# The order of nine query blocks, and where the masks of their selected keys are made

## What is computed

```
# per block of 128 queries, 8 heads that share one k and one v of width 64
score = sum_h wi[h] * relu(qi[h] . ki)          # the indexer
score = where(causal, score, -inf)
_, idx = top_k(score, 256)                       # each query keeps 256 keys
s = (q . k) / 8;  s = where(selected and causal, s, min)
p = softmax(s);   out = p @ v
```

## Time and profile before

| | |
|---|---|
| median of 3 runs | 4151.41 us (4147.45 to 4155.1) |
| the profiled execution | 4141.83 us, span 4140.0 us |
| PE busy | 3753.0 us, 91% of the span |
| DVE busy | 2171.5 us, 52% |
| ACT busy | 870.9 us, 21% |
| POOL busy | 555.9 us, 13% |
| attention, layer 0 | first score matmul at 472.2 us, last normalization ends at 625.7 |
| attention, layer 1 | first score matmul at 2511.2 us |

### The profile page before, as it was taken

One profiled execution on the slowest core, in us unless ns is written; L12 is line 12 of the kernel. 1 busy time (PEld: TensorE's weight loads), 2 busy tenths in 40 slices (PEclk: granted clock), 3 DMA queues, 4 the chain that ended last, 5 costly groups with the idle time before them and its releaser, 6 DMA issues.

```text
span 4140.0 us, 69037 instructions
## 1 busy us (share of the span) xinstructions
PE 3753.0 (91%) x29136; PEld 2849.3 (69%) x29136; DVE 2171.5 (52%) x4280; ACT 870.9 (21%) x1768; POOL 555.9 (13%) x444
## 2 busy tenths in 40 slices
PE   7999786999979999999889997769999799999995
PEld 4566464887548888888655664548865488888885
DVE  2599835666245243434646996366662542434345
ACT  1345463332010000000113445523320100000000
POOL 0041100000011221212100410000000121212220
PEclk9999897999889999999999998879998899999998
DMA  2001100000111111112210010100001111111121
GB/s 111 26 31 36 43 17 7 3 3 26 62 62 41 41 41 41 41 50 84 77 40 26 31 36 21 35 1 3 3 26 64 60 41 41 41 44 49 41 82 52
DMA packets 43383, 163.67 MB, mean 40 GB/s; under 512 B 5056, under 2 KB 5072, under 8 KB 42720
## 3 DMA queue, kind: packets, MB, share of 16 engines
q1 hardware_dynamic: 27648, 100.68, 7.0%
q0 software_dynamic: 15456, 58.85, 3.9%
HBM read 135.07 MB, written 23.49 MB: 38 GB/s over the span
## 4 chain that ended last, share of the span: by engine, by line
PE 71%; DVE 22%; issue 4%; ACT 2%; POOL 0%; DMA 0%; DVEq 0%; ACTq 0%; POOLq 0%
PE ps L708 38%; PE ps L738 7%; PE ps L657 7%; PE ps L625 6%; DVE arena L1421 5%; PE ps L899 2%; PE ps L887 2%; DVE little L1451 2%; PE ps L912 1%; PE ps L941 1%; DVE arena L1552 1%; PE ps L669 1%; PE ps L635 1%; DVE arena L1318 1%; DVE arena L1554 1%
## 5 line engine op out<-in xcount | busy, mean ns | idle before, releaser
L708 PE MATMUL ps<-arena 128*128 128x261 f32 x4096 | 924.7, 383 | 5.7 <-POOL arena L544 2.9
L708 PEld LDWEIGHTS ps<-arena 128*128 128x128 f32 x4096 | 775.1, 189 | 135.1 <-issue 5.4
L657 PE MATMUL ps<-arena,ring 128*128 128x348 f32 x2304 | 704.1, 465 | 37.4 <-DVE arena L1297 18.9
L708 PE MATMUL ps<-arena,ring 128*128 128x261 f32 x3072 | 705.1, 385 | 22.4 <-DVE arena L1774 22.1
L708 PEld LDWEIGHTS ps<-arena,ring 128*128 128x128 f32 x3072 | 584.2, 190 | 123.1 <-issue 21.3
L657 PEld LDWEIGHTS ps<-arena,ring 128*128 128x128 f32 x2304 | 438.8, 193 | 301.5 <-issue 59.2
L738 PE MATMUL ps<-arena 64*64 64x64 f32 (+1 forms) x13600 | 512.9, 226 | 97.6 <-DVE arena L1506 43.2
L738 PEld LDWEIGHTS ps<-arena 64*64 64x64 f32 x13600 | 467.6, 135 | 141.7 <-DVE arena L1552 48.8
L1276 ACT ACTIVATE aux<-ps 128x522 f32<-128x522 f32 x64 | 38.9, 607 | 1535.0 <-PE ps L708 1535.0
L1363 DVE TENSOR_TENSOR arena<-aux,ps 128x522 f32<-128x522 f32 x160 | 111.8, 699 | 423.1 <-PE ps L708 422.6
L544 POOL TENSOR_TENSOR arena<-ring 128x512 f32<-128x512 f32 x128 | 170.1, 1329 | 1106.9 <-DMA ring<-units 1101.5
(11 more groups left out here) (228 smaller groups left out, 3690.7 us busy)
## 6 DMA issues: line engine op xcount, KB each, us to landing
ring<-units SPq DMA_DIRECT2D x192, 512.0 KB, 3.7
h_scratch<-arena POOLq DMA_DIRECT2D x24, 522.0 KB, 3.2
arena<-h_scratch POOLq DMA_DIRECT2D x24, 522.0 KB, 8.1
arena<-h_in POOLq DMA_DIRECT2D x16, 522.0 KB, 10.2
out<-arena POOLq DMA_DIRECT2D x8, 522.0 KB, 3.1
arena<-att_scratch POOLq DMA_DIRECT2D x2, 2080.0 KB, 8.8
att_scratch<-arena POOLq DMA_DIRECT2D x16, 256.0 KB, 2.9
aux<-rope POOLq DMA_DIRECT2D x2, 1044.0 KB, 12.4
```

The lines of the kernel that those rows point to most:

```text
L657: ins = mm(ps[:, b + s, 0:SW], ring[:, r * D + k * P:r * D + (k + 1) * P], tile(U0, k)[:, slice_(s)], start=(k == 0), stop=(k == KT - 1))
L708: ins = mm(acc_at(n)[:, s], lhs[:, k * P:(k + 1) * P], rhs(k)[:, s * HALF:(s + 1) * HALF], start=(k == 0), stop=(k == KT // 2 - 1))
```

## The change

The masks of blocks 3 to 8 are made in the jobs of blocks 0 to 5, each three blocks ahead; only that of block 2 is made before attention. The jobs run over blocks 0 to 6, then 8, then 7. What went by a block's number (the bank for V and the spread, the place of the row sums, the counts in waits) now goes by its place in the sequence, and the numbers of row maxima done are summed over the jobs. POOL's copies of the mask of block 8 are issued between the stores of blocks 4 and 5 (before, between those of 3 and 4).

```
-        jobs = [(b, g) for b in range(packed) for g in range(4)] + [(packed, 0)]
-        SCORES = 2 * (len(jobs) - 1) + 1
+        sequence = [*range(packed - 1), packed, packed - 1]
+        place = {b: i for i, b in enumerate(sequence)}
+        jobs = [(b, g) for b in sequence for g in range(1 if b == packed else 4)]
         members = lambda b: range(1 if b == packed else 2)
-        ends = lambda u: 0 <= u < len(jobs) and (u + 1 == len(jobs) or jobs[u + 1][0] > jobs[u][0])
+        maxima = [sum(len(members(b)) for b, g in jobs[:u]) for u in range(len(jobs) + 1)]
+        SCORES = maxima[-1]
+        ends = lambda u: 0 <= u < len(jobs) and (u + 1 == len(jobs) or jobs[u + 1][0] != jobs[u][0])
...
-            return 2 * (u - 1) if jobs[u][0] < 4 else 2 * u
+            return maxima[max(u - 1, 0)] if jobs[u][0] < 4 else maxima[u]
...
-                for b in range(NQB):
+                for b in sequence:
                     n = rows(b)
-                    if b == 4:
+                    if b == packed - 3:
                         pool.wait_ge(S["mask_ready"], w.next("mask_ready"))
...
-                        if g == 0 and b >= 2:
-                            pe.wait_ge(S["att_out"], l * NQB + b - 1)
+                        if g == 0 and place[b] >= 2:
+                            pe.wait_ge(S["att_out"], l * NQB + place[b] - 1)
...
-                        if jobs[u - 2][0]:
-                            act.wait_ge(S["att_out"], l * NQB + jobs[u - 2][0])
+                        if u > 5:
+                            act.wait_ge(S["att_out"], l * NQB + place[jobs[u - 2][0]])
...
-                for b in range(FIRST_SEL, packed - 1):
-                    for step in range(7):
-                        make_mask(b, step)
+                for step in range(7):
+                    make_mask(FIRST_SEL, step)
...
-                        for h in (2 * g, 2 * g + 1) if b in (2, 3) else ():
-                            make_mask(packed - 3 + b, h)
-                        if (b, g) == (3, 3):
+                        if b + 3 <= packed:
+                            make_mask(b + 3, 2 * g)
+                            make_mask(b + 3, 2 * g + 1)
+                        if (b + 3, g) == (packed, 3):
                             dve.sem_inc(S["mask_ready"], 1)
...
-                        dve.wait_ge(S["prob_ready"], l * SCORES + (SCORES if b == packed else 2 * u))
+                        dve.wait_ge(S["prob_ready"], l * SCORES + maxima[u])
...
-                        if b or l:
-                            dve.wait_ge(S["att_stored"], 16 * (l * NQB + b))
+                        if place[b] or l:
+                            dve.wait_ge(S["att_stored"], 16 * (l * NQB + place[b]))
```

More of the change, by code:

```diff
@@ L898, in _ @@
                             for r in range(2):
-                                ins = mm(ps[HEAD * r:HEAD * (r + 1), 6 + b % 2, g * P:(g + 1) * P], val[0:kn, kb, :],
+                                ins = mm(ps[HEAD * r:HEAD * (r + 1), 6 + place[b] % 2, g * P:(g + 1) * P], val[0:kn, kb, :],
                                          pt(u, 0 if b == packed else r)[0:kn, kb, :], start=(kb == 0), stop=(kb == b))
@@ L922, in _ @@
                         pe.wait_ge(S["pt_out"], l * NTURN + turned + 1)
-                        sums = stat[:, 8 * (b % 2):8 * (b % 2) + 8]
+                        sums = stat[:, 8 * (place[b] % 2):8 * (place[b] % 2) + 8]
                         for g in range(1 if b == packed else 4):
@@ L1221, in _ @@
                         for r in members(b):
-                            c = 8 * (b % 2) + 2 * g + r
+                            c = 8 * (place[b] % 2) + 2 * g + r
                             x, at = sm[u % 2][r][:, 0:SEL_W[b]], 16 + 2 * (u % 2) + r
@@ L1650, in _ @@
                         b = jobs[u - 1][0]
-                        sums = stat[:, 8 * (b % 2):8 * (b % 2) + (1 if b == packed else 8)]
-                        dve.wait_ge(S["prob_ready"], l * SCORES + (SCORES if b == packed else 2 * u))
+                        sums = stat[:, 8 * (place[b] % 2):8 * (place[b] % 2) + (1 if b == packed else 8)]
+                        dve.wait_ge(S["prob_ready"], l * SCORES + maxima[u])
                         v.reciprocal(sums, sums).then_inc(S["inv_ready"], 1)
@@ L1664, in _ @@
                                     .rearrange("p (g r q) -> p g r q", r=2, q=n)[:, :, r]
-                                do(v.tensor_tensor(att_t[HEAD * r:HEAD * (r + 1), :, 0:n], own(ps[:, 6 + b % 2, 0:P]),
+                                do(v.tensor_tensor(att_t[HEAD * r:HEAD * (r + 1), :, 0:n], own(ps[:, 6 + place[b] % 2, 0:P]),
                                                    own(rinv[:, 0:P]), ALU.mult))
                         else:
-                            do(v.tensor_tensor(att_t, bank4(6 + b % 2), rinv.rearrange("p (g q) -> p g q", g=4),
+                            do(v.tensor_tensor(att_t, bank4(6 + place[b] % 2), rinv.rearrange("p (g q) -> p g q", g=4),
                                                ALU.mult))
```

## The result

Four executions of the changed kernel had a median of 4112.52 us (4112.0 to 4121.28), beside 4149.81 for four of the kernel before (4147.45 to 4155.1): ratio 0.9913, 95% interval 0.9897 to 0.9929. Faster was right; size and range were not. The profiled execution of the changed kernel took 4112.34 us, against 4141.83 before: 29.5 us less.

The account below looks back on a forecast made before the run. PE, idle 37.4 us before attention while DVE makes masks, was taken as the bound. Savings of 24.75, 2.4 and 0.4 sum to 27.5 us, from 4151.4 to 4123.9, rounded to 4124 (chance 0.68); range 4114 to 4135.

Parts of the forecast that it names:

- Part 1: PE's gap before attention: masks of blocks 3 to 6 leave it, start then set by POOL; 24.75 us less in all.
- Part 2: Six masks made inside attention, blocks 0 to 5: scores of (4, 0) 1.2 us earlier per layer, 2.4 us in all.
- L1644 of (1, 3): DVE's instruction in block 1 (L1641 before the change), queued behind mask steps and a normalization: about 1.5 us later.
- (b): Rival: DVE's masks not wholly hidden, jobs of blocks 0, 1, 4 and 5 become later; 4136 us, chance 0.13.
- (c): Rival: slower, attention latency-bound with every mask step between two L1641 on the path; 4177 us, chance 0.04.
- cover: DVE's idle time in blocks 4 and 5, 3.26 us before one L1641, to hide at most 2.6 us of steps.
- Part 3: End of attention, block 8 before block 7: net 0.2 us less per layer, 0.4 in all; bounds +2 to -2.
- the dip: Low clock around 518, after block 3 in layer 0 alone: costs 1.5 us, may go or come, zero in the sum.
- Rival (a): Clock stays high through the shorter gap, or the dip goes: at most 1.6 us per layer; 4119 us, chance 0.13.
- the base of the sum: Starting time for the whole kernel: median 4151.4 us of the runs shown, 9.6 above the profiled execution's 4141.8.
- runs of one kernel: Range term for the whole kernel's time: runs of one kernel lie 4 us from their median.

Follow-up runs that it names:

- e1: The kernel before, unchanged, timed and profiled again: 4144.09 us.
- e14: The kernel before with 11 matmuls of a constant added on PE behind attention in layer 0 alone: 4145.45 us.
- e4: The changed kernel again, no edit: 4119.31 us, ratio 0.9940.
- e11: The changed kernel for the third time, no edit: 4117.07 us, ratio 0.9933.
- e5: The changed kernel with masks 2, 3 and 4 made in the gap, 5 to 8 moved to other jobs: 4127.27 us, ratio 0.9949.
- e3: The kernel before with only the order changed, block 8 before block 7, masks made as before: 4147.37 us, ratio 1.0008.
- e2: The changed kernel with the jobs in the old order, block 8 last, so the mask change alone: 4124.43 us, ratio 0.9948.
- e6: The changed kernel with one unused 768-column DVE scan (1.8 us) more in each job of blocks 4 and 5: 4131.03 us, ratio 0.9961.
- e7: The changed kernel with 14 matmuls of a constant on PE in the gap before attention, both layers: 4126.05 us, ratio 0.9942.
- e12: The changed kernel with 6 constant matmuls in the gap before attention and 11 behind attention, both layers: 4113.69 us, ratio 0.9918.
- e15: The changed kernel with 6 constant matmuls in the gap before attention, and 11 behind attention in layer 0 alone: 4106.14 us, ratio 0.9905.
- e9: The changed kernel with 11 matmuls of a constant on PE behind attention, both layers: 4116.63 us, ratio 0.9928.

## Why the prediction was wrong in size, step by step

The cut of the profiles, in us, from starts of the same instructions. "Before" is the range of three profiles (first, e1, e14) and "changed" of three (first, e4, e11):

```
                                   before           changed         forecast
gap of PE, layer 0                 17.67 to 19.70   6.35            -11.45
gap of PE, layer 1                 19.67 to 19.68   6.35 to 6.36    -13.3
first scores to (4, 0), layer 0    44.25 to 44.71   42.09 to 43.26  -1.2
                        layer 1    43.21 to 44.39   41.29 to 42.49  -1.2
(4, 0) to attention's end, layer 0 107.59 to 109.06 107.07 to 107.09  -0.2
                           layer 1 107.58 to 107.80 107.08 to 107.09  -0.2
attention's end to L1715, layer 0  59.03 to 60.75   60.75 or 69.39   0
                          layer 1  83.72            83.72 to 83.73   0
```

(59.03 is e14's, with its filling.)

By the means of the three profiles each, the edited stretches, from PE's last projection tile to the end of attention in both layers, are 31.0 us shorter: 25.3 in the gaps, 3.6 up to (4, 0) and 2.1 behind it, for 24.75, 2.4 and 0.4. In the first pair of profiles they are 31.8 us shorter, and the stretches that nobody edited 2.3 longer, 2.1 of it from L1715 to the MLP of layer 0 (563.65 for 561.50); hence the 29.5 of the two spans.

**Part 1, the gap.** Right: 11.3 and 13.3 us, set by POOL and not by the masks' 25 us. e5 shows it by adding 10 us of masks, for which PE's gap grew by 0.2 us at most. In executions like e1's, where PE is 2 us sooner, the gain of layer 0 is 13.35; that case wasn't in the sum.

**Part 2, six masks inside.** Right in mechanism and nearly in size, 1.6 us per layer by the means with e3 and e2 taken in (44.3 to 42.7), 1.8 without them, for 1.2. What scatters these times is how long the low clock lasts into attention. With 10.0, 12.4, 13.3 and 15.7 us of it the changed kernel's are 41.29, 42.09, 42.49 and 43.23 us; before, with 10.1, 13.3 and 14.5 us, they are 43.20, 44.39 and 44.69. At equal length (10 or 13.3 us) the change is worth 1.9 us per layer. L1644 of (1, 3) was late by 1.8 us for a forecast 1.5, and blocks 2 and 3 gained it back. Blocks 4 and 5 cost nothing (107.08), so (b) and (c) fall. How much cover was left I overrated, and the form it takes I had wrong (of eight jobs one had none and two 0.18 us, but three more than 1.8): e6's 1.8 us per job cost 4.25 us per layer for the 1 forecast.

**Part 3, the order.** -0.5 to -0.7 us per layer for -0.2 (e2 against e3); small and of the right sign in the profiles, invisible in e3's total.

**The clock.** From (4, 0) to attention's end in layer 0 before took 109.06 us in its first profile and 108.93 in e14's, but 107.59 in e1's, and the changed kernel 107.07 to 107.09 in all three: the dip of before comes and goes, and is worth 1.4 us, as bounded. The clock's fall in the gap of before was read a little late: 0.69 in [459, 460] puts it at 459.4, 4.9 us into the gap, not at 459.7; nothing hangs on it. Rival (a), a clock kept high in blocks 0 and 1, didn't come about in the changed kernel. Its bound of 1.6 us per layer was too low: where e7 did keep the clock high, in layer 0, the scores of (4, 0) came 2.4 to 3.5 us sooner. The fillings lie on the same line as above: 40.77 and 40.80 us with 6.8 us of low clock (e12 and e15, layer 1), and 39.73 with none.

**The step that failed** is the base of the sum: "The median of the runs shown is 4151.4, 9.6 above the profiled execution, and the measured time goes by that". By the rows the changed kernel's profiled execution should have taken 4114.3; it took 4112.34. I had taken the 9.6 us for an offset of timing against profiling that both kernels have. The runs show no fixed one: the changed kernel's first profiled execution was 0.2 us under the median of its set, e1's 0.9 over, e4's at it and e11's 4.2 under. The base was a small sample that sat high, since e1's set gave 4143.5 for 21 executions of the same kernel, and the changed kernel's first four sat low (three at 4112).

The three sets with the changed kernel give 37.3, 24.2 and 30.8 us by medians, and 36.0, 25.4 and 28.4 by means. The means of all its 15 executions and of the 62 of before in the sets up to e12 are 4117.3 and 4145.7, 28.4 apart, for the forecast 27.5. Measured by them, the miss of 11.4 us (4123.9 against 4112.5) is 5.7 of base too high, 4.8 of the first four too low, and 0.9 of the sum.

The range allowed 4 us for "runs of one kernel", where the changed kernel alone covers 4111.8 to 4130.2; that term was too small by half or more. The bounds of parts 2 and 3 and of the dip, all added, would have given 4116.5 to 4132, which is wider than the 4119 to 4130 taken from them and still doesn't reach 4112.5.

That clock steps of 8.6 us (attention's end to L1715) and some 4 us (two later stages) make this spread is shown for the profiled executions. That they also made the first set of before high is inferred, and the chip is an untested rival, since the medians of before in the four later sets, each on another chip, go from 4143.5 to 4147.9. None of its executions above 4150 us left a profile; there is only a slightly lower mean clock in the results of that kernel (0.944 or 0.945 in executions of 4150.9 to 4155.2 us, 0.945 to 0.948 in those below 4146). Why the clock falls at one place in one execution and not in the next stays open, and so does why e3 and e5 stayed within 2.6 and 3.6 us where the changed kernel spread over 18; the fillings of e9 to e15 moved it and didn't fix it.

## What to carry to other kernels

Work taken out of a gap is worth only the distance to the next thing that the engine waits for. Read that one's end before costing the work, and then put other work there, which is free up to that point. Cover must be counted per job, from one instruction that the next stage needs to the following one, not per block. Where a change is worth under one per cent and PE has long half-idle stages, cut several profiles at the same instructions before believing either a median of four or the offset of one profile.

## What the runs showed of the hardware

Two things I hadn't expected. Identical code took 60.75 or 69.39 us in one stage, with a mean granted clock of 0.66 in the first profile and 0.57 in e4's, so PE was at 1.2 GHz for most of it in either case. After PE had been idle for 11.08 us, 24 instructions of 348 columns (12 float32 matmuls) took 14.27 us, at 0.50; they took 7.30, at 1.00, when PE had been kept busy with 11 matmuls of 512 columns (9.71 us). And a 512-column float32 matmul with constants shows as two instructions, together 0.87 us (12.18 us for 28, at 1.00), twice what I had sized it at.
